# Moving the norm of the last query tile from the handover into heads 0 to 4 of the attention

## The chip, the core and the metric

The kernel runs on one core of one Trainium2 chip. TensorE (PE) multiplies matrices, VectorE (DVE) and ScalarE (ACT) work element by element, GpSimd (POOL) fills and masks tiles, SyncE (SP) issues most transfers; each engine runs its own instructions in order and waits at semaphores for the others. The metric is the time of one execution on the device, in microseconds (us).

## What is computed

One inference step of a two-layer decoder in float32. 1024 prompt tokens with 16 meta tokens ahead of them (1040 rows) and 32 sample tokens (8 sequences of 4) go through a gated short convolution and a squared-ReLU MLP (layer 0), then through an attention with forget gates and a second MLP (layer 1). What matters here is the way from the query projection into the attention:

```python
q = rms_norm((xn @ w_q[j]).reshape(N, T, N_HEADS, HEAD_DIM), q_norm[j])
...
s = einsum('nqhd,nkhd->nhqk', q, k) * HEAD_DIM ** -0.5
s = s + (c_q - c_k)                    # c: running sum of log f, per head
s = where(k_pos <= q_pos, s, NEG_INF)
p = softmax(s, axis=-1)
o = einsum('nhqk,nkhd->nqhd', p, v)
```

There are 16 heads of 64 columns. Every query row is divided by the root mean square of its own 64 columns (`rms_norm` over the head), so that each tile of 128 columns holds two heads and needs two sums of squares per row.

## The kernel before

**Precision.** Each product is made of three: every operand is cut into a rounded high part and a low part, and PE multiplies high by high, low by high and high by low. ACT makes the high part (an activation with Copy, Exp or Square), DVE the low part (a subtraction).

**Query projection.** `unit` (L531) multiplies one tile of 128 columns of a weight with all 1074 token columns (three groups of 358), in eight steps of `k`; a dictionary `mid` hangs other work in front of a step. The eight query units are U_Q to U_Q + 7; U_O is the number that follows. For the query tile n, `scaled` (L2295, DVE) takes the result out of PSUM into `KW` with the token norm, ACT squares it twice (`head_squares`, L2132 and L2134), DVE makes the low part of the squares (`head_lo`, L2535), PE adds the squares of each head (`head_sums`, six products with `heads1`, the matrix `ones_per_head`, L569), ACT takes Ln of the three sums (L2146) and Exp with -0.5 (L2149), and DVE multiplies into the query tile `QS` (`head_fin`, L2541). Then the tile is staged: high part by ACT (`stage_hi`, L2140), low part by DVE (`stage_lo`, L2548), and both are stored to memory by SP (`stage_out`, L1888 and L1890), from where the heads load them (`load_head`, `load_cross`). Staging numbers count key tiles 0 to 7 and query tiles 8 to 15, so 14 and 15 are the last two query tiles, heads 12 to 15. The squares, sums and the product of tile n lie beside unit n + 1. The last tile has no unit behind it.

**Attention.** A head h has eight groups g of logits (NG = 8), and t = 8h + g counts all of them. PE's loop in `attention_tensor` does, at step t, `logits(t + 2)` (L1001, L1003) and `weigh_values(t)` (L1082 to L1084), and between the pieces of the latter the `uses` of the next head: 16 small products numbered 0 to 15 (`max_logits`, L923 to L936) for the row maxima, of which numbers 9, 11 and 15 ("A", "B", "C") turn the finished maxima of three row ranges into a row that ACT writes into the head's query tile (`keep_shift`, L975). They use PSUM banks 4 and 5 in turn (RING = 2), so number u waits until number u - 2 has been reduced. ACT's loop does `exp_logits(t)` (L1028 and L1033). DVE's loop does at step t `probs_lo(t + 1)` (L1045) and then `reduce_max` for the uses of step t (L947 to L968), `values_lo` (L1064) at g = 3, `invert_sums` (L1107) at g = 4 and `divide` (L1114) at g = 7. PE's `logits(t + 2)` waits for `exp_logits(t)`, and `weigh_values(t)` for `probs_lo(t)`. The head's diagonal blocks are reduced with `WIDE_MASK`; the second of these masks, which head 1 uses first at number 1, comes from POOL (`wide_mask(1)`, L1490 and L1492) behind `extend(1)`, four memsets at unit_done U_O and `extend(2)` (L1479 to L1485).

**The handover.** After the last unit PE does "C" of head 0, `logits(0)`, `logits(1)`, the six sums of tile 7, and only then enters the loop. ACT does the squares of tile 7 before `exp_logits(0)`, the roots after `exp_logits(1)`, then `stage_hi(14)`, the rounding of an output weight, and `stage_hi(15)`, which waits until the store of 14 is over (both use one buffer), and only then `exp_logits(2)`. DVE has `head_fin(14)`, `head_lo(15)` and five memsets of tail tiles ahead of `probs_lo(0)`, and `head_fin(15)`, `stage_lo(14)`, `cut_unit` and `stage_lo(15)` in steps 0 and 1.

The lines around which the change turns:

```python
for f in norm_sums.values():
    f()
pe.wait_ge(aux_read, AX_Q + 3 * KC)
pe.wait_ge(v_zero, 7)
for t in range(NG * HEADS):
    ...
    logits(t + 2)
    weigh_values(t, uses_of(h, g))
```

Of the kernel before, what the change touches and what calls it, by code (L numbers as in the profile page):

```python
# [154 lines left out]
USE_AT = [(0, 1), (2, 3), (4, 5), (6, 7), (8, 9), (10, 11), (12, 13), (14,)]  # L155
SHIFT_AT = {4: "A", 5: "B"}
# [17 lines left out]
def trunk(nc, a, out):  # L174

    ctx = ExitStack()
    with ctx:
# [133 lines left out]
        MASKED_ROW = [place("masked_first", [P, 512], offset=spare + 2048)[0]]  # L311
        C8, _ = place("minus_8_sums", [NH, NPR], offset=hid1 + slot * 6)
# [597 lines left out]
        def max_logits(h, u):  # L910
# [6 lines left out]
            ring_wait(h, u)  # L917
            if x in SHIFTS:
# [131 lines left out]

        def values_hi(h):
# [5 lines left out]
            act.activation(VH[:, hh, :, own], VRAW[:, :, own], ACT.Copy).then_inc(v_hi, 1)  # L1057

        def values_lo(h):

            _, hh = head(h)
            own, _ = halves(hh)
            dve.wait_ge(v_hi, h + 1)
            dve.tensor_tensor(VL[:, hh, :, own], VRAW[:, :, own], VH[:, hh, :, own].bitcast(F32), ALU.subtract)\  # L1064
               .then_inc(v_lo, 1)

        def weigh_values(t, uses=()):
# [8 lines left out]
            for c, j, q0, n, keys, bank, col in GROUPS[g]:  # L1076
# [12 lines left out]
                for use in uses[k:] if done else uses[k:k + 1]:  # L1089
                    if use:  # L1090
# [253 lines left out]
        def staged_in(n):  # L1344

            return 2 if n >= 2 * KC - 2 else n % 2
# [8 lines left out]
        def attention_loaders(stage_out):  # L1355
# [3 lines left out]
            def load_v(m):  # L1359
# [3 lines left out]
                sp.dma_start(VRAW[:, 0:NT - 1], vp[0:full, f].rearrange("(t p) c -> p t c", p=P)).then_inc(v_loaded, 16)  # L1363
                sp.dma_start(VRAW[0:LASTP, NT - 1], vp[full:NPR, f]).then_inc(v_loaded, 16)
# [36 lines left out]
            def attention_loads():  # L1401
# [4 lines left out]
                sp.wait_ge(unit_done, U_O)  # L1406
# [6 lines left out]
                stage_out(2 * KC - 2)  # L1413
                stage_out(2 * KC - 1)
# [3 lines left out]
                sp.wait_ge(z_fin, 2 * KC)  # L1418
                sp.wait_ge(st_kept[1], 32 * KC)
# [25 lines left out]
            def prompt_loads():  # L1445
                for h in range(HEADS):
# [9 lines left out]
                    for x in (0, 1, 2) if h == 0 else range(h + 2, min(h + 3, DB * NPAGE)):  # L1456
                        load_logf(x)
# [84 lines left out]
        def attention_scalar():  # L1542
            for t in range(2, NG * HEADS):
                exp_logits(t)
                h, g = divmod(t - 1, NG)
# [7 lines left out]
                if t == NG + 2:  # L1553
                    act.wait_ge(st_kept[1], 32 * KC)
# [71 lines left out]
        def attention_vector(head_fin, stage_lo):  # L1626

            probs_lo(0)
            dve.wait_ge(vo_ones, 4)
            values_lo(0)  # L1630
            for t in range(NG * HEADS):
# [3 lines left out]
                if t == 0:  # L1635
                    head_fin(2 * KC - 1, 1, G_QN, QS[:, KC - 1])
                    stage_lo(2 * KC - 2, QS[:, KC - 2, 0:NPR])
                if h + 1 < HEADS:
                    for u in USE_AT[g]:
                        reduce_max(h + 1, u)  # L1640
                    if g == 3:
                        values_lo(h + 1)
                if t == 1:
                    cut_unit(U_O + 1)
                    stage_lo(2 * KC - 1, QS[:, KC - 1, 0:NPR])
# [62 lines left out]

        def mask_rows():
# [1180 lines left out]
```

## Time and profile before

| | us |
|---|---|
| median of 3 runs | 2686.17 |
| lowest and highest of them | 2684.37 and 2688.18 |
| the profiled execution, its own time | 2688.92 |
| its span in the trace | 2686.7 |
| PE busy | 2633.2 |
| DVE busy | 1710.0 |
| ACT busy | 980.3 |

The profiled execution is 2.75 us above the median and 2.2 us above its own span. PE is busy for 98% of the span, so a change can shorten the time by taking away the little idle time of PE, or the stretches in which its granted clock is at half. The query projection ends and the attention begins near 1475 us; a head of the attention takes some 16.5 us.

### The profile page before, as it was taken

The page shows a single profiled execution, that of the slowest core. Times are in us where ns is not written, and L with a number is a line of the kernel's source. Part 1 is how long each engine was busy: PE and PEld are TensorE (multiplying, and loading weights), DVE is VectorE, ACT ScalarE, POOL GpSimd, SP SyncE. Part 2 cuts the span into 40 slices and gives each one's busy share as a digit, 9 for nine tenths or more (in the row PEclk, how much of TensorE's full clock was granted, in tenths as well). Part 3 has the DMA queues.
Part 4 walks back from the last instruction along what each step waited for, and adds up shares of the span by engine and source line. Part 5 has one row for each costly group of instructions (what it writes and reads, how often), then busy time and mean ns, then how long its engine had stood idle before and what let it go on. Part 6 is the DMA issues. An engine that isn't in the chain of part 4 may idle for free.

```text
span 2686.7 us, 48437 instructions
## 1 busy us (share of the span) xinstructions
PE 2633.2 (98%) x19052; PEld 2580.9 (96%) x19052; DVE 1710.0 (64%) x2621; ACT 980.3 (36%) x1555; POOL 25.6 (1%) x48
## 2 busy tenths in 40 slices
PE   8999999999999999999999899989999999999999
PEld 7999999999999999999999799978899999999999
DVE  5444447767666667744335788866686676767675
ACT  3111124323232323355245777755552222222222
POOL 0000000000000000000000100000000000000000
PEclk9999999999999999999999899999999999999999
DMA  3111110111111111124324556434211111111112
GB/s 115 48 47 40 47 54 35 48 47 47 47 47 47 47 47 47 48 79 153 105 75 145 145 132 164 108 119 155 86 56 40 55 39 55 39 55 39 55 39 81
DMA packets 208045, 193.05 MB, mean 72 GB/s; under 512 B 16208, under 2 KB 181008, under 8 KB 207938
## 3 DMA queue, kind: packets, MB, share of 16 engines
q1 hardware_dynamic: 188678, 182.50, 22.8%
q10 hardware_dynamic: 19260, 9.09, 1.2%
q8 instruction: 72, 1.18, 0.2%
q14 instruction: 35, 0.29, 0.0%
HBM read 160.93 MB, written 30.49 MB: 71 GB/s over the span
## 4 chain that ended last, share of the span: by engine, by line
PE 77%; DVE 3%; ACT 2%; issue 1%; DMA 0%; ACTq 0%; SPq 0%; DVEq 0%
PE ps L758 28%; PE ps L746 23%; PE ps L531 12%; PE ps L1082 2%; PE ps L1001 1%; PE ps L936 1%; PE ps L1083 1%; PE ps L1084 1%; PE ps L1003 1%; PE ps L1286 1%; PE ps L1128 1%; PE ps L569 1%; PE ps L632 0%; PE ps L1190 0%; DVE k_t_lo L1158 0%
## 5 line engine op out<-in xcount | busy, mean ns | idle before, releaser
L876 DVE TENSOR_TENSOR acc<-ps,acc 128x536 f32<-128x536 f32 x512 | 366.6, 717 | 254.7 <-PE ps L758 254.1
L758 PE MATMUL ps<-hidden_hi,w_hi 128*128 128x268 f32 x2048 | 423.5, 288 | 3.3 <-DVE hidden_lo L2425 1.7
L758 PE MATMUL ps<-hidden_hi,w_lo 128*128 128x268 f32 x2048 | 422.7, 288 | 0.0
L758 PE MATMUL ps<-hidden_lo,w_hi 128*128 128x268 f32 x2048 | 421.7, 287 | 0.0
L758 PEld LDWEIGHTS ps<-hidden_hi,w_hi 128*128 128x128 f32 x2048 | 321.2, 189 | 4.4 <-DVE hidden_lo L2425 2.1
L758 PEld LDWEIGHTS ps<-hidden_lo,w_hi 128*128 128x128 f32 x2048 | 322.4, 189 | 0.0
L758 PEld LDWEIGHTS ps<-hidden_hi,w_lo 128*128 128x128 f32 x2048 | 320.8, 189 | 0.0
L531 PE MATMUL ps<-x_hi,w_hi 128*128 128x358 f32 x1248 | 278.4, 331 | 4.5 <-DVE w_lo L515 4.5
L531 PE MATMUL ps<-x_hi,w_lo 128*128 128x358 f32 x1248 | 274.4, 328 | 0.0
L531 PE MATMUL ps<-x_lo,w_hi 128*128 128x358 f32 x1248 | 274.2, 328 | 0.0
L515 DVE TENSOR_TENSOR w_lo<-w_raw,w_hi 128x1024 fp32r<-128x1024 f32 x76 | 92.8, 1221 | 264.7 <-ACT w_hi L507 264.7
L531 PEld LDWEIGHTS ps<-x_hi,w_hi 128*128 128x128 f32 x1248 | 214.8, 191 | 6.4 <-DVE w_lo L515 4.9
L531 PEld LDWEIGHTS ps<-x_lo,w_hi 128*128 128x128 f32 x1248 | 217.1, 190 | 0.0
L531 PEld LDWEIGHTS ps<-x_hi,w_lo 128*128 128x128 f32 x1248 | 216.8, 190 | 0.0
L871 DVE TENSOR_TENSOR t<-ps,t 128x536 f32<-128x536 f32 x210 | 149.6, 713 | 62.6 <-PE ps L746 53.3
L507 ACT ACTIVATE w_hi<-w_raw 128x1024 fp32r<-128x1024 f32 x76 | 80.0, 1054 | 295.1 <-PE ps L531 287.3
L690 ACT ACTIVATE w_hi_a<-raw_a 128x512 fp32r<-128x512 f32 x30 | 19.0, 634 | 437.8 <-PE ps L746 437.8
L835 ACT ACTIVATE t<-t 128x536 f32<-128x536 f32 x120 | 78.3, 652 | 194.9 <-DVE t L851 194.2
L746 PE MATMUL ps<-x_hi,a_lo 128*128 128x268 f32 x720 | 148.3, 287 | 0.0
L746 PE MATMUL ps<-x_T_hi,s_lo 128*128 128x268 f32 x720 | 147.4, 286 | 0.0
L1045 DVE TENSOR_TENSOR probs_lo<-probs_f,probs_hi 128x768 fp32r<-128x768 f32 (+3 forms) x128 | 98.4, 769 | 34.4 <-ACT probs_hi L1033 18.9
L746 PEld LDWEIGHTS ps<-x_hi,a_lo 128*128 128x128 f32 x720 | 112.9, 189 | 0.0
(333 smaller groups left out, 5140.8 us busy)
## 6 DMA issues: line engine op xcount, KB each, us to landing
w_raw<-in_mlp_w SPq DMA_DIRECT2D x68, 512.0 KB, 4.0
raw_a<-in_mlp_w SPq DMA_DIRECT2D x120, 256.0 KB, 3.0
w_raw<-in_conv_w_in SPq DMA_DIRECT2D x24, 512.0 KB, 3.7
w_raw<-in_w_kv SPq DMA_DIRECT2D x16, 512.0 KB, 4.9
w_raw<-in_w_o SPq DMA_DIRECT2D x16, 512.0 KB, 4.1
k_page<-in_cache_k SPq DMA_DIRECT2D x16, 512.0 KB, 4.7
v_page<-in_cache_v SPq DMA_DIRECT2D x16, 512.0 KB, 4.6
kh_rows<-staged_hi SPq DMA_DIRECT2D x8, 520.0 KB, 2.7
```

The lines of the kernel that those rows point to most:

```text
L507: act.activation(WH[:, s], RAW[:, s], ACT.Copy).then_inc(w_hi, 1)
L515: dve.tensor_tensor(WL[:, s], RAW[:, s], WH[:, s].bitcast(F32), ALU.subtract).then_inc(w_lo, 1)
L531: mm = pe.matmul(PS[:, bank(s, g), 0:GW], w[:, s, k], x[:, k, g * GW:(g + 1) * GW], start=(k == 0 and n == 0), stop=(k == KC - 1 and n == 2))
L569: mm = pe.matmul(PS[:, b, 0:GW], weights[:, :], x[:, g * GW:(g + 1) * GW], start=not stop, stop=stop)
L746: mm = pe.matmul(PS[:, 2 * p + g, 0:QW], w[:, k], x[:, k, g * QW:(g + 1) * QW], start=(k == 0 and j == 0), stop=(k == KC // 2 - 1 and j == 2))
L758: mm = pe.matmul(PS[:, 2 * p + g, 0:QW], w[k][:, P * m:P * m + P], x[:, k, a:a + QW], start=(k == 0 and j == 0), stop=(k == 1 and j == 2))
L835: act.activation(UB[:, q % 2], UB[:, q % 2], ACT.Square).then_inc(hf_done, 1)
L871: dve.tensor_tensor(two(to), pair(p), two(other), ALU.add).then_inc(m_read, 1)
L876: dve.tensor_tensor(x, pair(p), x, ALU.add).then_inc(down_read, 1)
L936: mm = pe.matmul(PS[:, bank, 0:b - a], qa[:, q:q + rows], ck[:, a:b], start=True, stop=True)
L1045: dve.tensor_tensor(PBL[:, t % HI_RING, 0:nb * w], PF[:, t % 2, 0:nb * w], PBH[:, t % HI_RING, 0:nb * w].bitcast(F32), ALU.subtract).then_ ...
L1082: pe.matmul(to, VH[:, hh, j], ph, start=(j == 0), stop=False)
```

## The change

- The sums of tile 7 leave the handover. A new `late_norm(g)` does one third of them (two products) in the last step of heads 1, 2 and 3, in bank 5, behind use 13 of the next head; "C" of heads 2, 3 and 4 waits until ACT has read the third (`aux_read`).
- `logits(0)` moves into the last query unit, in front of its last step of `k`.
- ACT enters the attention right after the unit: `exp_logits(0)`, `values_hi(0)`, "C", `exp_logits(1)`. The Exp of tile 6 is at t = 3, `stage_hi(14)` at t = 5, the two squares of tile 7 at t = 7 and 11, the rounding of the output weight at t = 14, the three Ln at t = 17, 25 and 33, the Exp of tile 7 at t = 34, `stage_hi(15)` at t = 37.
- DVE: the memsets (`tail_ones`) at t = 2, `head_fin(14)` at t = 4, `stage_lo(14)` at t = 6, `head_lo(15)` at t = 12, `cut_unit` at t = 15, `head_fin(15)` at t = 35, `stage_lo(15)` at t = 38.
- Head 0 does the uses of head 1 as none at g = 0, then 0 to 2, 3 to 5, 6 and 7.
- Head 0's values are loaded into `OT` and not `VRAW`, before the unit is over, and tiles 14 and 15 have staging buffers of their own. SP stores them in its turns for heads 2 and 5; the loads of the log-f pages move from heads 0 to 13 into heads 5 to 12.

```diff
+USE_AT_FIRST = [(), (0, 1, 2), (3, 4, 5), (6, 7)] + USE_AT[4:]
+NORM_HEAD, NORM_BANK, NORM_USE = 1, 5, 13
...
             ring_wait(h, u)
+            if u == NORM_USE + RING and NORM_HEAD < h <= NORM_HEAD + G:
+                pe.wait_ge(aux_read, AX_Q + 3 * (KC - 1) + h - NORM_HEAD)
...
+        def attention_scalar(square, root, inverse, stage_hi):
+            act.wait_ge(unit_done, U_O)
+            exp_logits(0)
+            values_hi(0)
+            keep_shift(0, "C")
+            exp_logits(1)
             for t in range(2, NG * HEADS):
                 exp_logits(t)
+                h, g = divmod(t, NG)
+                if g == 1 and NORM_HEAD < h <= NORM_HEAD + G:
+                    root(AX_Q + 3 * (KC - 1) + h - NORM_HEAD - 1, NORM_BANK, h - NORM_HEAD - 1)
...
+                if t == 3:
+                    inverse(AX_Q + 3 * (KC - 1))
+                if t == 5:
+                    act.wait_ge(red_done, N_RED)
+                    stage_hi(2 * KC - 2, QS[:, KC - 2, 0:NPR])
+                if t == 7:
+                    act.wait_ge(v_lo, 2)
+                    square(U_Q, KC - 1, 0)
+                if t == 11:
+                    square(U_Q, KC - 1, 1)
+                if t == 14:
+                    round_unit(U_O + 1)
+                if t == NG * (NORM_HEAD + G) + 2:
+                    inverse(AX_Q + 3 * KC)
+                if t == NG * (NORM_HEAD + G) + 5:
+                    stage_hi(2 * KC - 1, QS[:, KC - 1, 0:NPR])
...
-                if t == 0:
-                    head_fin(2 * KC - 1, 1, G_QN, QS[:, KC - 1])
-                    stage_lo(2 * KC - 2, QS[:, KC - 2, 0:NPR])
...
+                if t == 2:
+                    tail_ones()
+                if t == 4:
+                    head_fin(2 * KC - 2, 0, G_QN, QS[:, KC - 2])
+                if t == 6:
+                    stage_lo(2 * KC - 2, QS[:, KC - 2, 0:NPR])
+                if t == 12:
+                    head_lo(U_Q, 2 * KC - 1, 1)
+                if t == 15:
                     cut_unit(U_O + 1)
+                if t == NG * (NORM_HEAD + G) + 3:
+                    dve.wait_ge(st_kept[0], 32 * KC)
+                    head_fin(2 * KC - 1, 1, G_QN, QS[:, KC - 1])
+                if t == NG * (NORM_HEAD + G) + 6:
                     stage_lo(2 * KC - 1, QS[:, KC - 1, 0:NPR])
...
+        def late_norm(g):
+
+            if g == 0:
+                pe.wait_ge(z_lo, 2 * KC)
+            pe.wait_ge(red_done, reds_through(NORM_HEAD + g + 1, NORM_USE))
+            c = slice(g * GW, (g + 1) * GW)
+            pe.matmul(PS[:, NORM_BANK, 0:GW], heads1[:, :], SQ[U_Q][1][1][:, c], start=True, stop=False)
+            pe.matmul(PS[:, NORM_BANK, 0:GW], heads1[:, :], T2R[:, c], start=False, stop=True).then_inc(aux_done, 1)
...
-        def attention_tensor(norm_sums):
-            first_max(KC - 1)
+        def first_logits():
+
             pe.wait_ge(unit_read, U_O - 1)
             logits(0)
+
+        def attention_tensor():
+            first_max(KC - 1)
             pe.wait_ge(unit_read, U_O)
             logits(1)
             pe.wait_ge(nm_kept, N_SH)
-            for f in norm_sums.values():
-                f()
-            pe.wait_ge(aux_read, AX_Q + 3 * KC)
-            pe.wait_ge(v_zero, 7)
```

On PE, before, at the end of the last query unit (L531), "C" of head 0 is L923 and `logits(0)` begins at the first L1001; the sums are L569:

```order
L531 MATMUL ps<-x_hi,w_lo 128x358 x3
L923 MATMUL ps<-ident,row_max 1x128 x2
L1001 MATMUL ps<-q_hi_ext_52,k_hi_ext_53 128x384
...
L1007 MATMUL ps<-ident,mask 128x256
...
L1003 MATMUL ps<-q_lo_hi_54,k_hi_lo_55 128x384
L569 MATMUL ps<-squares_r,ones_per_head 128x358
```

and in the changed kernel, in which L533 is the unit, L927 is "C", L1005 to L1013 are the logits and L1090 weighs the values:

```order
L1011 MATMUL ps<-ident,mask 128x256
L533 MATMUL ps<-x_hi,w_hi 128x358 x3
L533 MATMUL ps<-x_lo,w_hi 128x358 x3
L533 MATMUL ps<-x_hi,w_lo 128x358 x3
L927 MATMUL ps<-ident,row_max 1x128 x2
L1005 MATMUL ps<-q_hi_ext_52,k_hi_ext_53 128x384
...
L1013 MATMUL ps<-ident,mask 128x128
L1090 MATMUL ps<-probs_hi,v_hi 128x384
```

Eight products of `logits(0)` now stand in front of the last nine products of the unit, and no sum stands between `logits(1)` and the loop.

On ACT, before, from the Exp of tile 7 into the loop (L2140 is `stage_hi`, L507 the rounding of the weight):

```order
L2149 ACTIVATE t_84<-t_84 128x1074
L2140 ACTIVATE staged_hi_163<-q_all 128x1040
L507 ACTIVATE w_hi<-w_raw 128x1024
L2140 ACTIVATE staged_hi_163<-q_all 128x1040
L1028 ACTIVATE probs_f_155<-ps 128x768
L1033 ACTIVATE probs_hi<-ps 128x768
```

and in the changed kernel at t = 5 and 6 (L979 is `keep_shift`, L1110 `keep_chunk`, L2223 `stage_hi(14)`, L1032 and L1037 are `exp_logits`):

```order
L979 ACTIVATE q_hi_ext_56<-ps 1x400
L1110 ACTIVATE o_and_sums<-ps 128x384
L2223 ACTIVATE staged_hi_150<-q_all 128x1040
L1032 ACTIVATE probs_f_158<-ps 128x544
L1037 ACTIVATE probs_hi<-ps 128x544
L979 ACTIVATE q_hi_ext_56<-ps 1x384
```

`stage_hi(14)` stood ahead of the loop and stands now between "A" of head 1 and `exp_logits(6)`.

On DVE, before, from the low part of the first probabilities on (L2541 is `head_fin`, L2548 `stage_lo`):

```order
L1045 TENSOR_TENSOR probs_lo<-probs_f_155,probs_hi 128x768
L1064 TENSOR_TENSOR v_lo<-v_raw,v_hi 128x9x64
L1045 TENSOR_TENSOR probs_lo<-probs_f_155,probs_hi 128x768
L2541 SCALAR_TENSOR_TENSOR q_all<-k_work,vectors,t_84 128x1074
L2548 TENSOR_TENSOR staged_lo_164<-q_all,staged_hi_163 128x1040
L947 TENSOR_REDUCE max_parts<-ps 128x2
```

and in the changed kernel at t = 4 and 5 (L1049 is `probs_lo`, L963 to L972 reduce, L2623 is `head_fin(14)`):

```order
L1049 TENSOR_TENSOR probs_lo<-probs_f_158,probs_hi 128x544
L963 ISA masked_next,max_parts<-ps,mask_wide_next 128x272
L963 ISA max_parts 128x1
L972 TENSOR_REDUCE row_max<-max_parts 128x3
L2623 SCALAR_TENSOR_TENSOR q_all<-k_work,vectors,t_84 128x1074
L1049 TENSOR_TENSOR probs_lo<-probs_f_158,probs_hi 128x544
L967 TENSOR_REDUCE max_parts<-ps 128x1
```

`head_fin(14)` stood ahead of the loop and stands now between the reduction of use 8 and `probs_lo(6)`.

## Rows read from the trace of the kernel before

**Rows 1.** The page of the profile: busy time of each engine

```profile
PE 2633.2 (98%) x19052; PEld 2580.9 (96%) x19052; DVE 1710.0 (64%) x2621; ACT 980.3 (36%) x1555; POOL 25.6 (1%) x48
```

**Rows 2.** Table by stretch: start:end, length, then busy us (x instructions) of PE, PEld, DVE, ACT, POOL; clock

```profile
1475.50:1510.60 35.10, 25.07 (x140) 22.13 (x138) 23.14 (x49) 23.11 (x39) 8.86 (x12) 0.81 0.56 161
1528.00:1545.00 17.00, 16.88 (x126) 16.10 (x125) 14.88 (x38) 12.49 (x25) 0.00 (x0) 1.00 0.57 133
```

**Rows 3.** Timeline of PE, handover: start, duration, engine, line, shape, [idle before <- ended by]

```profile
1477.00 0.45 PE L1001 MATMUL ps<-q_hi_ext,k_hi_ext 128*128 128x384 f32 x1 [0.25 <-DVE k_work L2295]
...
1480.80 0.64 PE L569 MATMUL ps<-squares_r,ones_per_head 128*128 128x358 f32 x1 [2.83 <-issue]
...
1494.54 0.36 PE L1001 MATMUL ps<-q_hi_ext,k_hi_ext 128*128 128x272 f32 x1 [2.45 <-ACT probs_hi L1033]
...
1499.57 0.38 PE L1082 MATMUL ps<-probs_hi,v_hi 128*128 128x256 f32 x1 [1.77 <-DVE probs_lo L1045]
```

**Rows 4.** Table by stretch, PE alone: start:end, length, busy, granted clock (1.00 is full)

```profile
1480.00:1490.00 10.00, 6.95 (x26) 0.51 0.76 195
1500.00:1504.00 4.00, 4.00 (x22) 0.57 0.90 256
1306.00:1308.00 2.00, 2.00 (x9) 0.50 0.58 174
```

**Rows 5.** Timeline of PE, a gap ahead of the attention

```profile
1305.13 1.24 PE L632 MATMUL ps<-ident,k_work 128*128 128x128 f32 x6 [2.66 <-DVE k_work L2295]
```

**Rows 6.** Timeline of DVE, handover

```profile
1475.73 1.21 DVE L2295 TENSOR_TENSOR k_work<-ps,rms_inv 128x1074 f32<-128x1074 f32 x1
...
1486.66 1.34 DVE L2541 SCALAR_TENSOR_TENSOR q_all<-k_work,vectors,t 128x1074 f32<-128x1074 f32 x1 [2.17 <-ACT t L2149]
1487.92 1.24 DVE L2548 TENSOR_TENSOR staged_lo<-q_all,staged_hi 128x1040 fp32r<-128x1040 f32 x1
```

**Rows 7.** Timeline of ACT, handover

```profile
1485.53 1.10 ACT L2149 ACTIVATE t<-t 128x1074 f32<-128x1074 f32 x1
...
1491.92 1.07 ACT L2140 ACTIVATE staged_hi<-q_all 128x1040 fp32r<-128x1040 f32 x1 [3.39 <-DMA ql_rows<-staged_lo]
```

**Rows 8.** Timeline of POOL, the masks and head 2's tiles

```profile
1385.46 0.62 POOL L1492 TENSOR_SCALAR_AFFINE_SELECT mask_wide_first<-mask_wide_first 128x512 f32<-128x512 f32 x1
...
1478.93 0.96 POOL L1479 MEMSET k_hi_ext<- 64x1040 f32 x1
...
1483.68 1.28 POOL L1492 TENSOR_SCALAR_AFFINE_SELECT mask_wide_next<-mask_wide_next 128x512 f32<-128x512 f32 x1
```

**Rows 9.** Timeline of PE inside the attention, heads 1 and 2

```profile
1513.88 0.34 PE L1082 MATMUL ps<-probs_hi,v_hi 128*128 128x384 f32 x1
...
1521.46 0.39 PE L1082 MATMUL ps<-probs_hi,v_hi 128*128 128x272 f32 x1
...
1523.00 0.41 PE L1001 MATMUL ps<-q_hi_ext,k_hi_ext 128*128 128x384 f32 x1
...
1530.41 0.34 PE L1082 MATMUL ps<-probs_hi,v_hi 128*128 128x384 f32 x1
```

**Rows 10.** Timeline of DVE inside the attention, head 1

```profile
1520.69 0.72 DVE L1045 TENSOR_TENSOR probs_lo<-probs_f,probs_hi 128x544 fp32r<-128x544 f32 x1
1521.33 0.43 DVE L959 CUSTOM_DVE_ANT_0 masked_next<-ps,mask_wide_next 128x272 f32<-128x272 f32 x1
...
1522.95 0.73 DVE L1045 TENSOR_TENSOR probs_lo<-probs_f,probs_hi 128x544 fp32r<-128x544 f32 x1 [0.83 <-ACT probs_f L1028]
...
1529.05 0.94 DVE L1045 TENSOR_TENSOR probs_lo<-probs_f,probs_hi 128x768 fp32r<-128x768 f32 x1
```

**Rows 11.** Timeline of ACT inside the attention, head 1

```profile
1520.82 0.49 ACT L975 ACTIVATE q_hi_ext<-ps 1x400 fp32r<-1x400 f32 x1 [1.71 <-PE ps L923]
...
1522.23 0.63 ACT L1033 ACTIVATE probs_hi<-ps 128x544 fp32r<-128x544 f32 x1
...
1528.90 0.37 ACT L975 ACTIVATE q_hi_ext<-ps 1x256 fp32r<-1x256 f32 x1 [1.21 <-PE ps L923]
```

More of the change, by code:

```diff
@@ L311, in trunk @@
         MASKED_ROW = [place("masked_first", [P, 512], offset=spare + 2048)[0]]
+        for name, offset in (("staged_hi2", spare), ("staged_hi3", ot0)):
+            STH.append(place(name, [P, NPR], F32R, offset=offset)[0])
+        STL += 2 * [place("staged_lo2", [P, NPR], F32R, offset=kw0)[0]]
         C8, _ = place("minus_8_sums", [NH, NPR], offset=hid1 + slot * 6)
@@ L1056, in values_hi @@
             ge(act, pv_done, NG * (h - 1))
[L1057 removed]
+            act.activation(VH[:, hh, :, own], v_raw(m)[:, :, own], ACT.Copy).then_inc(v_hi, 1)
         def values_lo(h):
[L1061 removed]
+            m, hh = head(h)
             own, _ = halves(hh)
             dve.wait_ge(v_hi, h + 1)
[L1064 removed]
+            dve.tensor_tensor(VL[:, hh, :, own], v_raw(m)[:, :, own], VH[:, hh, :, own].bitcast(F32), ALU.subtract)\
                .then_inc(v_lo, 1)
@@ L1089, in weigh_values @@
                 for use in uses[k:] if done else uses[k:k + 1]:
-                    if use:
+                    if isinstance(use, int):
+                        late_norm(use)
+                    elif use:
                         max_logits(*use)
@@ L1624, in past_copy, with attention_vector @@
                 act.activation(EX[:, :], EXF[:, :], ACT.Copy).then_inc(ex_ready, 1)
-        def attention_vector(head_fin, stage_lo):
+        def attention_vector(head_lo, head_fin, stage_lo):
             probs_lo(0)
-            dve.wait_ge(vo_ones, 4)
+            dve.wait_ge(vo_ones, 2)
             values_lo(0)
@@ L2226, in _ @@
             round_unit(U_Q + 2)
-            for n in range(KC):
-                if n == KC - 1:
-                    keep_shift(0, "C")
+            for n in range(KC - 1):
                 head_squares(U_Q, n)
-                if n == KC - 1:
-                    exp_logits(0)
-                    values_hi(0)
-                    exp_logits(1)
-                elif n:
+                if n:
                     stage_hi(KC + n - 1, QS[:, n - 1, 0:NPR])
@@ L2662, in _ @@
                     cut_unit(U_Q + n + 2)
-            attention_vector(head_fin, stage_lo)
+            attention_vector(head_lo, head_fin, stage_lo)
             for m in range(KC):
@@ L2858, in norm, with end @@
                     f()
-                unit(U_Q + n + 1, mid={**mid, 6: norm, 7: sums[7]})
-            attention_tensor(head_sums(U_Q, 1, ax(AX_Q + 3 * (KC - 1), 0, 0), 2 * KC - 1))
+                def end(n=n, f=sums[7]):
+                    f()
+                    if n == KC - 2:
+                        first_logits()
+                unit(U_Q + n + 1, mid={**mid, 6: norm, 7: end})
+            attention_tensor()
             eight(U_OS, 0, HH, HL, sample_ready, groups=(2,), bank=lambda s, g: G * s)
```

116 lines of the change are left out of this document (67 added, 49 removed).

## The prediction

> **What bounds the kernel now.** I read the page first, then PE's idle times over the span, then the timelines of PE, ACT, DVE and POOL from 1475 us on, then one undisturbed head of the attention. The page says PE is busy for 2633.2 of 2686.7 us [rows 1], so the whole idle time of PE is 53 us, and a change that removes no products can win only there or where PE's clock is at half.
>
> The largest single place of both is the one that is changed. From 1475.5 to 1510.6 PE is busy for 25.07 of 35.10 us [rows 2]: 10.0 us idle, four pieces of it 0.25, 2.83, 2.45 and 1.77 us [rows 3]. The 2.83 is the wait for the squares of tile 7, the 2.45 the wait for `exp_logits(2)`, which ACT reaches only after `stage_hi(15)`, and that waited 3.39 us for the store of tile 14 [rows 7]; the 1.77 is DVE doing `cut_unit` and `stage_lo(15)`. The granted clock is at half, 1.2 GHz, for the 10 us from 1480 and for most of the 4 us from 1500 [rows 4]. In the first PE worked 6.95 us at 0.51, in the second 4.0 us at 0.57, so 6.95 x 0.49 + 4.0 x 0.43 = 5.1 us of that work would not be there at 2.4 GHz. The handover thus costs 10.0 + 5.1 = **15.1 us**. No more than that is to be had.
>
> In an undisturbed head everything is full: over 17.0 us PE 16.88, DVE 14.88, ACT 12.49 [rows 2], at full clock; a head takes 1530.41 - 1513.88 = 16.53 us from one place to the same place of the next [rows 9]. DVE has 2.1 us a head to spare, ACT 4.4.
>
> **Part 1, sums of tile 7.** The six products take the same time wherever they stand, so their busy time cancels. Their waits (2.83 us, and 2.25 more before the second pair and `logits(2)`) go. In heads 1 to 3 their operands have been ready since t = 12, and ACT's Ln, about 0.5 us, falls into its idle time ahead of "C" (1.21 us, [rows 11]). I take 0 for the new waits; if "C" did have to wait, 3 x 0.5 us.
>
> **Part 2, what is late next on PE.** `logits(0)`, 1.1 us by its like at 1523.00 to 1524.1 [rows 9], used to fill PE while DVE took the last unit out of PSUM, and PE then lacked only 0.25 us [rows 3]. DVE's 1.21 us [rows 6] still have to pass between the end of the unit and `logits(1)`, which writes the same banks. With `logits(0)` inside the unit nothing is left to cover them but "C": a wait of **1.4 us** takes the place of the 0.25.
>
> **Part 3, head 0 and the second mask.** ACT now starts its exps at the end of the unit, so PE can enter step 0 near 1479.2 (unit end 1476.6, "C", the wait, `logits(1)`) and would reach use 3 of head 1 at about 1484.6, adding up the steps of head 1 in the timeline. Use 3 needs bank 5 from use 1, whose reduction needs `WIDE_MASK[1]`. POOL's queue ahead of it does not move: `extend(2)` from 1478.93, the mask ready at 1484.96 [rows 8], or 0.1 later. `reduce_max(1, 1)` and with it `probs_lo(3)`, queued behind it on DVE, start there: PE waits 0.85 us at use 3, and, since DVE is then one step behind and has uses 3, 4, 5 and the memsets (some 0.5 us) in step 2, 0.7 us at use 5, 0.35 at step 4 and 0.2 at step 5. Together **2.1 us**. Before, this cost nothing as all were late anyway.
>
> Here a page bears on a term. `WIDE_MASK[1]`'s select took 1.28 us, the first mask's 0.62 [rows 8]; the slow one ran beside `probs_lo`, with both inputs in SBUF, the fast one beside a DVE instruction with one of them in PSUM. By the Trainium skill, "GPSIMD Engine Reference", Key points, GpSimd shares its SBUF interfaces with VectorE and contends with instructions that have two SBUF inputs; the trace agrees. In the changed kernel DVE would stand waiting at that moment, and by that rule the mask comes 0.65 us sooner, this term would be 1.5, not 2.1, and the time 2683.2.
>
> **Part 4, the loop at t = 4 to 6.** This is the largest new wait. `stage_hi(14)` at ACT's t = 5 waits for `head_fin(14)`, which DVE does at the end of its step 4, and `exp_logits(6)` is queued behind it on ACT; for that wait both `logits(8)` on PE and `probs_lo(6)` on DVE. In head 1 of the trace the reduction of use 8 starts at 1521.33 [rows 10] and with its join is done at 1521.96. `head_fin` takes 1.34 us less its overlap, 1.25 [rows 6]: 1523.2. `stage_hi` 1.05 [rows 7]: 1524.3. Two exps of 544 columns (0.63 each, 1.05 together) [rows 11]: 1525.35. PE wants `logits(8)` at 1523.00 [rows 9]. So it waits 2.35 us, and with head 0's slightly shorter DVE step **2.5 us**. Lower bound 0.5, if DVE is ahead by two steps; it cannot be below nothing, since all these are additions to queues that are in use.
>
> **Part 5, the rest of DVE's and ACT's pieces.** What DVE can take without holding PE up is the distance of the end of `probs_lo(t)` to `weigh_values(t)`: for g = 5 it ends where the next instruction starts, 1521.33, against 1521.46, 0.1 us; for g = 1 it ends at 1529.9 against 1530.41, 0.5 us [rows 9, 10]; for g = 0 it is some 0.9. The single pieces are 1.2 us (`stage_lo`, `cut_unit`, `head_lo` as `stage_lo`) and 1.25 [rows 6].
> - t = 6 and 7 (`stage_lo`, the first square): 0.15 us.
> - t = 11 and 12: DVE stands idle for 0.83 us before `probs_lo` of g = 6 [rows 10] and ACT for 1.71 us before "A" [rows 11], so nothing.
> - t = 14 and 15: the rounding pushes `probs_lo(15)` and the steps behind it by 1.07 us, `cut_unit` adds 1.15, in front of `divide`, against 0.5 us before `weigh_values(17)`: **1.8 us**.
> - t = 34 to 38: the Exp of tile 7 (1.10, [rows 7]) pushes `probs_lo(35)` by 0.45, `head_fin(15)` comes right before `probs_lo(37)`, g = 5: 1.55 us; `stage_lo(15)` and the `divide` behind it another 0.75. **2.3 us**. The ACT piece at t = 37 hides in the delay that is there by then.
>
> Sum 4.3 us, bounds 1 (only the g = 5 case) and 6 (each of the five DVE pieces at full length). The SP edits cost nothing: the head loads are issued a head ahead of their use, the stores stand behind them in SP's turns, and the log-f pages are first read in head 15.
>
> **Part 6, the clock.** After a gap of 2.66 us the clock was at half [rows 4, 5], after the 2.83 too, and after the pair of 2.45 and 1.77 again [rows 3, 4]. The changed kernel has one gap of 2.5 us and two clusters of 1.5 and 2. I expect one stretch like that from 1500 (1.7 us lost), and half a chance of another: **2.3 us**; bounds 0 and the 5.1 us of now.
>
> **Sum.** 15.1 - 1.4 - 2.1 - 2.5 - 0.1 (ACT's "C") - 4.3 - 2.3 = 2.4 us faster. Against the profiled execution's own 2688.92 that is 2686.5; the median of the runs is 2.75 lower, 2686.17, so I forecast **2683.8 us**. About 0.2%, 5.4 us, is what a measurement of this kernel can tell from no change.
>
> **Rivals.**
> *The pieces hide.* If DVE and ACT run further ahead than the timeline of head 1 shows, most of parts 4 and 5 are absorbed by their 2.1 and 4.4 us a head, the gaps stay short and the clock stays up: 15.1 - 1.4 - 2.1 - 0.5 - 1 - 0.5 = 9.6 us faster, 2676.6. For it: spare time per head exceeds the pieces, 2.8 us on DVE in head 0 with no `divide` in it. Against it: the 0.1 us at g = 5, and the loop through both engines in part 4.
> *The clock eats it (slower).* Gaps near 2 us now come at steps 2, 6, 17 and 37, and each could hold PE at half clock for as long as after 1480, 10 us of stretch, or 3.4 us lost each time: 4 x 3.4 = 13.6 in place of 2.3, so 15.1 - 10.4 - 13.6 = 8.9 us slower, 2695.1. It decides from about three long stretches on. Against it: after the 2.45 and 1.77 gaps the stretch was only 4 us long [rows 4], and a slower PE lets DVE catch up.
> *The late sums wait.* "C" of heads 2 to 4 waits for ACT's Ln, and `late_norm` for the reduction of use 13, which DVE does last in its step 6. At 1 us each the gain is gone: 2686.8. Against it: in head 1 that reduction is over 0.6 us before the place of `late_norm`. This would be the case where stalls were only moved.
>
> **Chances.** The forecast, with its bounds from 2681 to 2688: 0.54. Pieces hide: 0.32, nearly all of it faster by over 5.4 us. Clock: 0.08. Late sums: 0.06, no change. So faster 0.31, same 0.60, slower 0.09. For 8 in 10 the range takes in most of the first rival and leaves the second out: 2677 to 2689.
>
> **What would show it.** PE, at the end of the unit: one wait of 1.4 us ended by DVE's `k_work` (L2377 now); then no product of `ones_per_head` before heads 1, 2 and 3. POOL's mask ends near 1485 and PE's first wait on DVE's reductions in the bank of use 3 stands right there. At t = 6 a gap of 2 to 2.5 us before `logits(8)`, ended by ACT's `exp_logits(6)`, with `staged_hi` waiting for DVE ahead of it. Waits of 1 to 2 us near `weigh_values(17)` and `weigh_values(37)`. PE's step 8 some 8 us sooner than now (7.1 of gain by then, 1.0 because the sums come later). If those waits are missing, part 5 is wrong and the time nears 2677; if the clock shows 0.5 in three or more places behind 1476, the second rival holds. A wait at "C" of heads 2 to 4 would be the third.

## The result and the profile after

| | before | changed |
|---|---|---|
| median of 20 runs each, us | 2685.61 | 2690.07 |
| lowest and highest | 2684.07 and 2688.18 | 2686.19 and 2693.22 |
| the profiled execution's own time | 2688.92 | 2690.25 |
| its span | 2686.7 | 2688.0 |

The changed kernel takes 1.0017 times as long, 95% interval 1.0011 to 1.0024: 3.0 to 6.4 us slower. I had said 2.4 us faster and a range that ended at 2689.

The page of the changed kernel hardly tells them apart: PE is busy for 2633.1 us in it, for 2633.2 in [rows 1].

So I put marks on PE's timeline: the first use of each head, the pair of 128x16 products of L928 before and L932 now. These two rows of the changed kernel (start, duration) are the first uses of heads 6 and 7. PE does them when it begins heads 5 and 6, so head 5 took 1590.92 - 1574.07 = 16.85 us:

```profile
1574.07 0.28 PE L932 MATMUL ps<-k_hi_ext,q_hi_ext 128*128 128x16 f32 x2
...
1590.92 0.28 PE L932 MATMUL ps<-k_hi_ext,q_hi_ext 128*128 128x16 f32 x2
```

From mark to mark, in us (the second trace of the changed kernel is experiment 5's):

| stretch | before | changed | changed, second trace |
|---|---|---|---|
| first use of head 0 to the end of head 0 | 88.52 | 79.49 | 79.10 |
| heads 1 to 5 | 82.78 | 89.22 | 87.72 |
| heads 6 to 12 | 116.36 | 123.04 | 124.36 |
| together | 287.66 | 291.75 | 291.18 |

The 4.1 us between the first two columns fit the medians, which are 4.5 us apart. The two profiled executions as a whole differ by only 1.3 us, since this execution of the kernel before was 2.8 us longer outside these stretches; only the marks are compared here.

The handover did give about what I said: 9.0 us. Heads 1 to 5 gave 6.4 back, of which some 1.0 are the six products that moved there (an estimate: 0.17 us from one product of this shape to the next in a unit). Then heads 6 to 12, in which the change puts no piece of the norm on PE, ACT or DVE, took 6.7 more: head 6 took 21.75 us and head 9 18.49, the other heads from 7 on 16.5 to 16.6 as before. (In the second trace head 6 took 21.93 and heads 7, 8 and 9 took 17.07, 17.39 and 17.90.) That is the part that turned the sign.

PE's timeline of the changed kernel shows where it stood (start, duration, line, shape, then idle time before and what ended it); these rows answer to [rows 3] and [rows 9]:

```profile
1476.19 0.44 PE L1005 MATMUL ps<-q_hi_ext,k_hi_ext 128*128 128x384 f32 x1 [1.32 <-DVE k_work L2377]
...
1484.86 0.50 PE L940 MATMUL ps<-k_hi_ext,q_hi_ext 128*128 128x512 f32 x1 [0.39 <-DVE max_parts L963]
...
1493.66 0.41 PE L1005 MATMUL ps<-q_hi_ext,k_hi_ext 128*128 128x384 f32 x1 [2.65 <-ACT probs_hi L1037]
...
1521.36 0.41 PE L1090 MATMUL ps<-probs_hi,v_hi 128*128 128x384 f32 x1 [0.75 <-DVE probs_lo L1049]
...
1564.27 0.39 PE L1090 MATMUL ps<-probs_hi,v_hi 128*128 128x272 f32 x1 [1.22 <-DVE probs_lo L1049]
...
1601.95 0.45 PE L1005 MATMUL ps<-q_hi_ext,k_hi_ext 128*128 128x384 f32 x1 [0.72 <-DMA k_hi_lo<-kl_rows]
...
1605.77 0.40 PE L1090 MATMUL ps<-probs_hi,v_hi 128*128 128x272 f32 x1 [2.51 <-DVE probs_lo L1049]
...
1658.89 0.39 PE L1090 MATMUL ps<-probs_hi,v_hi 128*128 128x272 f32 x1 [0.60 <-DVE probs_lo L1049]
```

The first five are the waits of parts 2 to 5 of the prediction. The sixth and seventh are head 6, the last is head 9. The view that groups waits names what stood behind the 2.51 and the 0.60 us on DVE (engine, instruction, what it waited for: us in total, times, longest), in the attention of the changed kernel:

```profile
DVE inv_spread L1117 <- DMA sums_spread<-o_and_sums: 9.9, 7, 4.6
```

Before, this was 0.4 us, once. DVE's row of the longest, which `probs_lo` is queued behind:

```profile
1604.88 0.25 DVE L1117 RECIPROCAL inv_spread<-sums_spread 65x16 f32<-65x16 f32 x1 [4.57 <-DMA sums_spread<-o_and_sums]
```

`sums_spread` is the transfer that brings the sums of the head just finished to `invert_sums`. SP issues it in the turn of the next head, behind eight loads for the two heads to come; behind it in the same turn stand the transfers of the inverted sums, V, the stores and the pages. SP's timeline in the changed kernel, from the end of the turn of head 5 into that of head 6 (start, duration of the issue, line, destination <- source):

```profile
1586.22 0.42 SPq L1966 DMA_DIRECT2D ql_rows<-staged_lo  x1
1593.49 1.49 SPq L1447 DMA_DIRECT2D logf_page<-in_cache_logf  x2
1595.02 0.47 SPq L1392 DMA_DIRECT2D q_lo_hi<-ql_rows  x1
...
1596.97 0.60 SPq L1392 DMA_DIRECT2D k_hi_lo<-kl_rows  x1
...
1600.08 0.87 SPq L1400 DMA_DIRECT2D sums_spread<-o_and_sums  x1
```

and the same place before (L1439 is now L1447, L1389 is L1400):

```profile
1591.43 0.39 SPq L1439 DMA_DIRECT2D logf_page<-in_cache_logf  x1
...
1597.52 0.87 SPq L1389 DMA_DIRECT2D sums_spread<-o_and_sums  x1
```

Against the mark of head 6, which had just begun on PE (1595.36 before, 1590.92 now) `sums_spread` is issued 2.2 us behind it before and 9.2 us behind it now. DVE had its turn for the sums 9.4 us behind the mark before, and they landed 4.8 us after their issue now, so there was little to give away. The load of `k_hi_lo` for head 7 came late by the same cause: PE stood 0.72 us for it. SP's waits in the same stretch say why:

```profile
SPq L1469 <- DMA ql_rows<-staged_lo: 5.8, 1, 5.8
```

This is `sp.wait_ge(st_kept...)`: the stores of tile 15 (520 KB each) must have landed before anything loads from them. They are first read by the loads of head 14, but SP is one queue, and two log-f pages, the loads of heads 7 and 8 and the sums of head 5 stood behind the wait. Head 9 is a smaller case of it: DVE stood 2.23 us for `sums_spread`. The turn ahead of it loads a V block, two log-f pages and a K page; so do the turns ahead of heads 7 and 11, which took 16.53 and 16.57 us here but 17.76 and 17.32 in `a_wait_turn6`. Why it is one head in one trace and another in the next was not worked out.

### The profile page after: what moved, and what is told of

It is laid out like the page before. It is cut to its first block and busy times, and to the rows that moved or that the text cites. A ratio compares the mean times of both kernels' runs of the same rounds, so it can differ in the third digit from the quotient of the medians.

```text
span 2688.0 us, 48443 instructions
## 1 busy us (share of the span) xinstructions
PE 2633.1 (98%) x19052; PEld 2578.7 (96%) x19052; DVE 1710.3 (64%) x2622; ACT 981.4 (37%) x1555; POOL 24.9 (1%) x48
## 5 line engine op out<-in xcount | busy, mean ns | idle before, releaser
L533 PE MATMUL ps<-x_hi,w_hi 128*128 128x358 f32 x1248 | 278.2, 331 | 4.3 <-DVE w_lo L517 4.3
L533 PE MATMUL ps<-x_lo,w_hi 128*128 128x358 f32 x1248 | 273.9, 328 | 0.0
L533 PE MATMUL ps<-x_hi,w_lo 128*128 128x358 f32 x1248 | 273.5, 327 | 0.0
L533 PEld LDWEIGHTS ps<-x_hi,w_hi 128*128 128x128 f32 x1248 | 214.5, 190 | 6.2 <-DVE w_lo L517 4.8
L533 PEld LDWEIGHTS ps<-x_lo,w_hi 128*128 128x128 f32 x1248 | 217.1, 190 | 0.0
L533 PEld LDWEIGHTS ps<-x_hi,w_lo 128*128 128x128 f32 x1248 | 216.0, 189 | 0.0
L1049 DVE TENSOR_TENSOR probs_lo<-probs_f,probs_hi 128x768 fp32r<-128x768 f32 (+3 forms) x128 | 98.2, 767 | 26.4 <-ACT probs_hi L1037 9.5
```

What stands on the lines that cost most here:

```text
L533: mm = pe.matmul(PS[:, bank(s, g), 0:GW], w[:, s, k], x[:, k, g * GW:(g + 1) * GW], start=(k == 0 and n == 0), stop=(k == KC - 1 and n == 2))
L1049: dve.tensor_tensor(PBL[:, t % HI_RING, 0:nb * w], PF[:, t % 2, 0:nb * w], PBH[:, t % HI_RING, 0:nb * w].bitcast(F32), ALU.subtract).then_ ...
```

## The experiments

Theory 1: SP's queue makes heads 6 and 9 long, by the wait for the stores and by the log-f pages that come in pairs. Theory 2, its rival: the pieces of the norm on ACT and DVE leave a debt that comes due there. All intervals are 95%, against the kernel before on the same chip.

### 1. Take away one suspect each

`a_wait_turn6`, the changed kernel with SP's wait and the start of the log-f pages a turn later; the stores stay where they are:

```diff
                     if h == 5:
                         stage_out(2 * KC - 1)
+                    if h == 6:
                         sp.wait_ge(st_kept[0], 32 * KC)
                         sp.wait_ge(st_kept[1], 32 * KC)
-                    if 5 <= h < 5 + DB * NPAGE // 2:
-                        load_logf(2 * h - 10)
-                        load_logf(2 * h - 9)
+                    if 6 <= h < 6 + DB * NPAGE // 2:
+                        load_logf(2 * h - 12)
+                        load_logf(2 * h - 11)
```

> The changed kernel with one edit on SP: the wait for the store of tile 15 and the loads of the log-f pages begin in SP's turn for head 6, not 5. Theory 1 (SP's queue): in the changed kernel SP waits 5.8 us in turn 5 for the store and then spends 2.5 us on the first two pages, so that the loads of the next turn and with them the sums of head 5 come late; DVE stands 4.6 us idle for them and head 6 takes 21.75 us where 16.55 is usual. Then this kernel gets back about 5 us: some 2685, head 6 at 16.6 to 17.5 us. Theory 2 (the pieces on ACT and DVE): DVE carries a debt from heads 0 to 4 and SP only shows it; then the time stays within 1 us of the changed kernel's 2690 and the idle time moves to another head.

Measured: 2685.99 us, ratio 0.9999 (0.9990 to 1.0008). Head 6 took 16.58 us instead of 21.75, head 9 still 18.61: heads 6 to 12 took 119.95 us, with heads 7 and 11 now 1.2 and 0.7 us over 16.6. SP did not wait for the stores at all, as they had landed by then. The edit gave 4.1 us by the medians (taken on two chips; 4.8 by the two ratios). Since the stores still stand in turn 5, it is not their traffic that made head 6 long.

`a_stage_t6`, the changed kernel with `stage_hi(14)` on ACT at t = 6:

```diff
-                if t == 5:
+                if t == 6:
                     act.wait_ge(red_done, N_RED)
                     stage_hi(2 * KC - 2, QS[:, KC - 2, 0:NPR])
```

> The changed kernel with one edit on ACT: the high part of tile 14 is made at t = 6, behind exp_logits(6), and not at t = 5 in front of it. Both theories: the 2.65 us gap of PE in front of logits(8) shrinks to under 0.5 us and the stretch of 4 us at half clock behind it is gone (1.7 us), so head 0 is 3.5 to 4.3 us shorter. Theory 2 says that this is most of what was lost: 2686. Theory 1 says that head 6 still takes over 20 us, and the time is 2686 to 2687 all the same: head 6 tells them apart, not the time.

Measured: 2688.89 us, ratio 1.0008 (0.9999 to 1.0017). The stretch to the end of head 0 went from 79.49 to 76.64 us, but head 6 still took 22.61 and DVE still stood 4.75 us for `sums_spread`. So the loop at t = 5 and 6 is real and costs 2.4 to 2.8 us (2.40 of the 2.85 us are in head 0 itself), and head 6 is long without it. The time came out above the 2686 to 2687 that both theories had: heads 6 to 12 took 124.23 us, 1.2 more than in the changed kernel's trace.

### 2. Put the suspect into the kernel before

`b_logf_pairs` has the kernel before load its log-f pages two a turn in turns 5 to 12; nothing else is changed.

```diff
-                    for x in (0, 1, 2) if h == 0 else range(h + 2, min(h + 3, DB * NPAGE)):
-                        load_logf(x)
+                    if 5 <= h < 5 + DB * NPAGE // 2:
+                        load_logf(2 * h - 10)
+                        load_logf(2 * h - 9)
```

> The kernel before with one edit on SP: the log-f pages are loaded two a turn in turns 5 to 12, not three in turn 0 and one a turn from 1 on. Theory 1: a part of the loss in heads 6 to 9, as the turns get 0.8 us longer where the k pages are loaded as well: 0 to 2 us slower than the kernel before. Theory 2: no change, within 0.5 us.

Measured: 2689.31 us, ratio 1.0011 (1.0002 to 1.0020). That is 3.0 us slower (0.5 to 5.4), a little over the 0 to 2 of theory 1. Heads 6 to 12 took 119.78 us against 116.36, with head 9 at 18.49 us as in the changed kernel, but head 6 at 16.64: the pages alone do not make head 6 long.

`b_sp_side` is `b_logf_pairs` with two stores of 520 KB (into a tensor `extra_rows` that nothing reads) and a wait for them in turn 5, ahead of the pages:

```diff
+                    if h == 5:
+                        for x in range(2):
+                            sp.dma_start(extra_rows[x], QS[:, KC - 1, 0:NPR]).then_inc(gate_w_loaded, 16)
+                        sp.wait_ge(gate_w_loaded, 48)
```

> The kernel before with the whole of SP's turn 5 put in: two stores of 520 KB each (of a query tile into a scratch tensor, so with no work on ACT, DVE or PE), the wait until both have landed, and the log-f pages two a turn in turns 5 to 12. Theory 1: head 6 is 3 to 5 us longer than 16.6, with DVE idle for sums_spread, and the kernel 3 to 6 us slower than before. Theory 2: no change, within 0.5 us.

Measured: 2695.32 us, ratio 1.0028 (1.0017 to 1.0039), 7.5 us slower by the ratio and more than the 3 to 6 expected. Its wait on SP and DVE's row in head 6:

```profile
SPq L1439 <- DMA extra_rows<-q_all: 6.4, 1, 6.4
```

```profile
1609.03 0.25 DVE L1108 RECIPROCAL inv_spread<-sums_spread 65x16 f32<-65x16 f32 x1 [5.20 <-DMA sums_spread<-o_and_sums]
```

Head 6 took 23.16 us and head 9 20.64. The kernel before has none of the moved pieces, and it shows the long heads of the changed one. Theory 2 falls as the cause of heads 6 and 9; theory 1 holds from both sides. By these traces the pages are worth 3.4 us (119.78 - 116.36) and the stores with their wait 7.7 more (127.44 - 119.78) in heads 6 to 12; by the medians it is 2.8 and 6.0, and the execution of `b_sp_side` that was traced was its slowest, 2698.63 us. The wait without the pages was not run.

### 3. All of SP's side mended

`c_sp_only`, the changed kernel with the wait in turn 6 and one log-f page behind it, and the others three a turn in turns 10 to 14, in place of the pairs from turn 5:

```diff
+                    if h == 6:
+                        sp.wait_ge(st_kept[0], 32 * KC)
+                        sp.wait_ge(st_kept[1], 32 * KC)
+                        load_logf(0)
+                    if 10 <= h < 15:
+                        for x in range(3):
+                            load_logf(3 * h - 29 + x)
```

> The changed kernel with its SyncE side alone rearranged: the wait for the stores of tile 15 moves from turn 5 to turn 6, the log-f pages start with one page in turn 6 and go on with three a turn in turns 10 to 14 instead of two a turn from turn 5. Theory 1 (SyncE's queue held up the next head's rows in the turn of head 5 and in the turns that also load a K page and a V block) expects heads 6, 7 and 9 to take 16.6 us each (21.75, 16.5 and 18.5 in the changed kernel), so about 5 + 1.9 = 7 us less than the changed kernel's profiled time and half a us to a clock step besides: about 2683 to 2684 us, some 2 us under the kernel before. Theory 2 (the pieces of the norm on ScalarE and VectorE leave a debt that comes due in heads 6 and 9) expects those heads to stay at 18 to 22 us and the time at 2688 or above. Head 0 stays at 20 to 21 us and head 4 at 19 to 20 us by both.

Measured: 2683.07 us, ratio 0.9989 (0.9980 to 0.9998). Heads 6 to 12 took 115.98 us, every one of them 16.5 to 16.6. DVE's reciprocal (L1117) in head 6 waits for nothing there.

With SP out of the way the change is 2.4 us faster than before by the medians (0.5 to 5.4 by the interval). What I had forecast, 2683.8, is the time of this kernel and not of the changed one.

### 4. The pieces on the other engines

`d_stage6` is `c_sp_only` with `stage_hi(14)` on ACT at t = 6, as in `a_stage_t6`.

> c_sp_only with one piece moved: the high half of tile 14 is staged on ScalarE at t=6 and not at t=5. If the loop of my prediction (that piece ahead of the exponentials of a step) costs what the trace shows, TensorE's wait of 2.64 us and the stretch at half clock behind it go, and head 0 takes 18.3 us (19.8 in c_sp_only): 1.5 us off, about 2681 us. If a piece only hands its wait on, head 0 stays at 19.8 us or head 1 takes 1 us more than 17.45.

Measured: 2681.51 us, ratio 0.9979 (0.9969 to 0.9988). To the end of head 0 it took 76.98 us against 79.73, heads 1 to 5 stayed at 87.74 (87.75). The wait did not move on. I had expected 1.5 us and it gave 2.75.

`c_moved` is `d_stage6` with five other pieces and the mask moved as well:

```diff
             pool.wait_ge(unit_read, U_O)
-            extend(2)
             wide_mask(1)
+            pool.wait_ge(p_wide, 2)
+            extend(2)
...
-                if t == 14:
+                if t == 19:
                     round_unit(U_O + 1)
-                if t == NG * (NORM_HEAD + G) + 2:
+                if t == NG * (NORM_HEAD + G) + 3:
                     inverse(AX_Q + 3 * KC)
-                if t == NG * (NORM_HEAD + G) + 5:
+                if t == NG * (NORM_HEAD + G) + 6:
                     stage_hi(2 * KC - 1, QS[:, KC - 1, 0:NPR])
...
-                if t == 15:
+                if t == 20:
                     cut_unit(U_O + 1)
-                if t == NG * (NORM_HEAD + G) + 3:
+                if t == NG * (NORM_HEAD + G) + 4:
                     dve.wait_ge(st_kept[0], 32 * KC)
```

> The kernel above with the pieces of the norm and of the staging put where the trace of the changed kernel shows their engines ahead: the first half of the last two staging steps and the inverse of tile 15 one step later on ScalarE, the two pieces of rounding and cutting five steps later, and GpSimd's second mask filled ahead of the last zeroing of V's tail. Theory 1 with the loop of my prediction (a piece in ScalarE ahead of the exponentials that TensorE needs next) expects head 0 at about 17 to 18 us instead of 20.7, the wait of 0.75 us for the probabilities at t=17 gone, the wait for the second mask gone, and head 4 at 17 to 19 us: 2679 to 2681 us, 5 to 7 us under the kernel before. The rival (the wait only moves on to the next piece, and the half-clock stretch is set by the handover itself) expects head 0 at 18.3 us but heads 1 and 4 longer by as much, and 2683 to 2684 us.

Measured: 2679.49 us, ratio 0.9976 (0.9966 to 0.9985). Heads 1 to 5 took 87.02 us. PE has three waits of 0.3 us or more from the loop's start to head 6, 0.56, 0.43 and 0.78 us, all for `probs_lo`.

`d_no_mask` is `c_moved` without the edit on POOL, the engine that makes the mask.

> c_moved with GpSimd's second mask behind the last zeroing again. If the mask sets the start of head 0 (VectorE waited 1.45 us for it in a_stage_t6 and 0.2 us or less in c_moved), head 0 takes 18.3 us again (17.1 in c_moved) and heads 1 to 4 are as in c_moved: 1.2 us above c_moved, about 2680.5 us. If the masks are hidden behind the loads and the ones in the extended rows, head 0 stays within 0.3 us of 17.1 and the other moved pieces (at t=19, 20 and in head 4) are what gave c_moved its gain over d_stage6.

Measured: 2678.47 us, ratio 0.9970 (0.9956 to 0.9984); it cannot be told from `c_moved`. Head 0 did take 18.32 us with a wait of 1.46 us for the mask on DVE, as expected if the mask decides, but it began 1.56 us sooner (experiment 5 says why), so that the stretch to the end of head 0 was 76.66 us against 77.00.

`c_moved_l0` is `c_moved` with `logits(0)` behind the query unit again.

```diff
-                def end(n=n, f=sums[7]):
-                    f()
-                    if n == KC - 2:
-                        first_logits()
-                unit(U_Q + n + 1, mid={**mid, 6: norm, 7: end})
+                unit(U_Q + n + 1, mid={**mid, 6: norm, 7: sums[7]})
...
         def attention_tensor():
             first_max(KC - 1)
+            first_logits()
```

> The kernel above with the first logits taken out of the last query unit again and put behind it. If moving them into the unit is worth what my prediction says (they fill TensorE while it waits for nothing, so they only change places), the time is within 0.7 us of the kernel above; if the early first logits are what brings the handover gain, head 0 starts 1 us or more later and the time is 1 to 2 us above it. The mark of head 0 against the end of the last query unit tells the two apart.

Measured: 2677.21 us, ratio 0.9971 (0.9959 to 0.9982). To the end of head 0 it took 77.22 us (77.00): moving the first logits into the unit only changed their place, and PE's wait at the handover is 0.25 us for DVE and 1.41 us for ACT's "C" instead of 1.33 us for DVE. This is the fastest version that ran, 0.29% under the kernel before and below both kernels; `c_moved` and `d_no_mask` are within its interval.

### 5. Is the clock at the handover the program's?

In five of the eight traces of the changed kernel and its variants the granted clock fell to half behind PE's wait of 1.3 to 1.4 us at the handover, and three show the same wait without a fall. Two kernels were run once more, unchanged.

> c_moved once more, unchanged, for its trace. After TensorE's wait of 1.33 us at the handover the granted clock fell to half in c_moved, c_moved_l0, d_stage6, c_sp_only and a_wait_turn6 and stayed at full in the changed kernel, a_stage_t6 and d_no_mask. If the drop belongs to the program (what stands around the wait), it is at half here again and head 0 starts 59.9 us after the mark ahead of it. If it belongs to the single execution, it may stay at full: then head 0 starts at 58.3 us, and since the second mask is ready early here, head 0 still takes 17.1 us, 1.5 us less in all than in any trace so far.

> The changed kernel once more, unchanged, for its trace. If the clock at the handover belongs to the program, it stays at full again (58.8 us to head 0, a wait of 1.2 us for the second mask, head 0 of 20.7 us). If it belongs to the single execution, it may fall: 59.9 us to head 0, no wait for the mask, head 0 of 19.8 us. By both the wait of 2.65 us at t=6 and the long heads 6 (21.8 us) and 9 (18.5 us) come back, since SyncE's queue makes them.

`c_moved` and then its second trace, by stretch (start:end, length, busy us and instructions of PE, PEld, DVE, ACT, POOL, then the clock, DMA share, GB/s):

```profile
1476.00:1480.00 4.00, 4.00 (x19) 4.00 (x19) 2.53 (x3) 3.48 (x6) 3.68 (x5) 0.58 0.95 213
```

```profile
1476.00:1480.00 4.00, 3.56 (x23) 3.24 (x23) 2.81 (x4) 3.95 (x7) 3.62 (x7) 1.00 0.87 210
```

The same program ran these 4 us at 0.58 once and at 1.00 once; the loop's first mark came 59.90 and 58.33 us behind the first use of head 0. So this fall is not fixed by the program. With it the mask is settled too: at full clock moving it is worth 76.66 - 75.57 = 1.1 us (`d_no_mask` against the second trace of `c_moved`), and at half clock nothing: head 0 took 17.09 us in `d_stage6`, with the mask late, and 17.10 in `c_moved`. The changed kernel's second trace kept the clock at full at the handover, had the wait of 2.66 us at t = 6 again, and head 6 at 21.93 us. Two numbers missed what was expected of full clock: head 0 took 19.86 us, not 20.7, since PE stood 0.75 us for the rows of head 1 ahead of the loop's first mark (0.29 in the first trace) and met the mask later, and head 9 took 17.90 us, not 18.5.

## Why the prediction was wrong

**The step that failed** is the last paragraph of part 5: "The SP edits cost nothing: the head loads are issued a head ahead of their use, the stores stand behind them in SP's turns". The stores do; but the wait for the stores stands in SP's queue ahead of the next turn's transfers, and `sums_spread`, the ninth of them, has no head of slack: it is issued when a head has begun and is used in that head, at g = 4. Nor are all the head loads a head ahead: the four of `load_cross` for head 7 were issued in head 6 and PE stood 0.72 us for one of them. And that the log-f pages are first read in head 15 says nothing of the time that their issue takes in front of these transfers. I had asked who reads what, and not what is queued behind it on SP. It cost 6.7 us in heads 6 to 12 (8.0 in the second trace) where the sum has 0, and experiment 3 takes all of it back. Without it the number came out: `c_sp_only` took 2683.07 us, 2.4 below the kernel before, as forecast. That the two agree so closely is partly luck, since two terms were wrong in opposite directions (parts 3 and 6 below) and the interval is 0.5 to 5.4 us.

**The handover.** Forecast was 8.1 us by PE's step 8, measured 9.03 (9.42 in the second trace), 0.9 more, with part 3 too high and a clock term that falls in this stretch.

**Part 1** holds: there is no wait at "C" of heads 2 to 4 in the trace, so the rival of the late sums was not the case.

**Part 2** holds: 1.32 us, ended by `k_work`, for 1.4.

**Part 3** was too high: DVE waited for the mask, but PE lost nothing at use 3 and only 0.39 us at use 5, not 2.1 in all. By experiment 5 the mask's whole price is 1.1 us at full clock. I let DVE's delay of one step run on through steps 2 to 5; the waits at steps 4 and 5 are not in the trace, and why they are not was not worked out. DVE's wait and POOL's select:

```profile
1482.90 0.31 DVE L963 CUSTOM_DVE_ANT_0 masked_next<-ps,mask_wide_next 128x144 f32<-128x144 f32 x1 [1.18 <-POOL mask_wide_next L1507]
```

```profile
1482.16 0.61 POOL L1507 TENSOR_SCALAR_AFFINE_SELECT mask_wide_next<-mask_wide_next 128x512 f32<-128x512 f32 x1
```

The select that took 1.28 us in [rows 8] took 0.61 now, while DVE stood waiting for it, and 0.61 to 0.66 in every other trace, also in `b_logf_pairs`, where the `probs_lo` ahead of it ended 0.12 us after its start. By the Trainium skill, "GPSIMD Engine Reference", Key points, GpSimd shares its SBUF interfaces with VectorE and contends with its instructions that have two SBUF inputs; these traces agree.

**Part 4** holds: 2.65 us for 2.5, in the very chain that was added up. ACT's rows of it, `stage_hi(14)` and the two exps of `exp_logits(6)`:

```profile
1491.42 1.07 ACT L2223 ACTIVATE staged_hi<-q_all 128x1040 fp32r<-128x1040 f32 x1 [1.51 <-DVE q_all L2623]
1492.39 0.61 ACT L1032 ACTIVATE probs_f<-ps 128x544 f32<-128x544 f32 x1
1492.90 0.62 ACT L1037 ACTIVATE probs_hi<-ps 128x544 fp32r<-128x544 f32 x1
```

Taking the piece one step later removed it, at no cost in heads 1 to 5 (experiments 1 and 4).

**Part 5** in its other terms: nothing at t = 6 and 7 (0.15 forecast), 0.75 us at `weigh_values(17)` for 1.8, and 1.22 us at g = 5 of head 4, with some 0.85 in four small waits behind it, for 2.3. Heads 1 to 5 together lost 6.4 us in one trace and 4.9 in the other, some 1.0 of it the moved products, against 4.3 and the part of the clock that falls there. The two traces differ by 1.5 us in head 4 alone, in which the second one shows full clock. So the size of the term holds, but not its parts.

**Part 6, the clock.** I allowed 2.3 us. The changed kernel's trace has three stretches below full:

```profile
1494.00:1498.00 4.00, 4.00 (x19) 3.90 (x18) 2.65 (x7) 3.42 (x8) 0.00 (x0) 0.57 1.05 234
...
1564.00:1572.00 8.00, 7.58 (x42) 7.24 (x43) 5.58 (x14) 6.14 (x12) 0.00 (x0) 0.79 0.58 147
1604.00:1612.00 8.00, 6.23 (x30) 5.86 (x31) 5.46 (x13) 3.03 (x4) 0.00 (x0) 0.79 0.40 103
```

By busy time and clock they hold 4.00 x 0.43 = 1.7, 7.58 x 0.21 = 1.6 and 6.23 x 0.21 = 1.3 us: 4.6, the third of them behind the wait that SP made; without it 3.3, 1.0 over the term. Three stretches are what I had named as the sign of the rival "the clock eats it", but each is 3 to 4 us of half clock, as after 1500 in [rows 4], and not 10; that rival, 2695.1 us, had two of its four places right (steps 6 and 37) and the price too high. "The pieces hide", 2676.6 us, was not the case of this kernel, but is near what `c_moved_l0` reached once each piece stood where its engine had room.

## What to carry to other kernels

A wait in a queue that issues transfers is paid by whatever is issued next and used soonest, so list for every such wait the transfers behind it with their own slack, also those that have nothing to do with it; put it where what it waits for has landed: one turn later SP no longer waited at all. When a piece moves into a full loop, a step earlier or later can decide between some 2.7 us and nothing: find the instruction queued behind it that another engine wants next. Where a measured gain at the place of the change does not arrive in the total, mark the same instruction in every later turn of the loop and look for the turn that grew.

## What was not expected of the hardware

- Two stores of 520 KB, issued at 1585.58 and 1586.22, had SP waiting for 5.8 us behind the second, and in `b_sp_side` 6.4; the page's median from issue to landing for the eight stores `kh_rows` of the same 520 KB is 2.7 us. What they shared the transfer engines with in this turn was not tried.
- A log-f page, whose number SP reads from a table first, takes SP longer than its issue. One log-f page took 0.39 us for the issue and SP stood some 1.0 to 1.25 us ahead of it (before, in turns 4 to 6); a pair took 1.49 us with 1.1 us ahead of it (the wait ended near 1592.4, the issue began at 1593.49). So the second page of a turn costs SP about a further 1.1 us. In a queue in which `sums_spread` has no slack the pairs were worth 3.4 us over heads 6 to 12 in the trace of `b_logf_pairs`.
- After a wait of 1.3 to 1.4 us at the handover the granted clock fell to half in five traces and stayed at full in five others, and the same program did both. In `c_moved_l0` that wait was ACT's 1.41 us, in the nine others DVE's 1.32 or 1.33. A clock stretch behind a wait of this length cannot be read from one trace as the effect of an edit.
